# Order of weight splits in a two-stack transformer kernel: feed-forward slab 23, attention's projection slabs, a table load

## What is computed

```python
def swiglu(h, norm_g, w_in, w_out):
    u = rmsnorm(h, norm_g)
    gu = u @ w_in
    return (jax.nn.silu(gu[..., :FFN_HIDDEN]) * gu[..., FFN_HIDDEN:]) @ w_out
...
    for l in range(DEPTH):
        sh_a, sc_a, g_a, sh_f, sc_f, g_f = jnp.split(silu_c @ mod_w[l] + mod_b[l], 6, axis=-1)
        a_lat = modulate(h_lat, sh_a, sc_a)
        o_lat, o_ctx = even_mixer(...)   # l == 0: latent attention and neighbourhood attention, one projection
        # l == 1: odd_mixer, attention in windows with sinks
        h_lat = h_lat + g_a * o_lat
        h_lat = h_lat + g_f * swiglu_2(modulate(h_lat, sh_f, sc_f), ffn_w_gate_up[l], ffn_w_down[l])
```

## Time and profile before

| what | us |
|---|---|
| median of three runs | 3265.7 |
| the three runs | 3265.70, 3267.14, 3250.51 |
| profiled execution | 3255.09 |
| its span | 3253.2 |
| TensorE matmul busy | 3019.9 (93%) |
| VectorE busy | 1637.6 (50%) |
| ScalarE busy | 1157.6 (36%) |
| GpSimd busy | 263.6 (8%) |
| mean granted TensorE clock | 0.967 |

### The profile page before, as it was taken

How to read it: one execution, slowest core, us unless ns; L and a number is a source line. 1 busy time by engine, 2 the same in 40 slices (tenths; PEclk the granted TensorE clock), 3 DMA queues, 4 the chain that set the end, 5 groups by cost and what they waited for, 6 DMA issues and landing times.

```text
span 3253.2 us, 39195 instructions
## 1 busy us (share of the span) xinstructions
PE 3019.9 (93%) x15560; PEld 2529.4 (78%) x15560; DVE 1637.6 (50%) x2743; ACT 1157.6 (36%) x1927; POOL 263.6 (8%) x220
## 2 busy tenths in 40 slices
PE   7899999887888999999798999999999989999998
PEld 5678887665777788878577887888888779878887
DVE  6756665656675667651345754222222545343333
ACT  3532223434673222241345743211112345432222
POOL 2310001000561000010000100000000000000001
PEclk9999999898999999999899999999999989999999
DMA  3235444241002445431000011211121110023231
GB/s 139 85 109 162 155 156 149 75 152 34 1 1 85 149 156 175 145 120 49 33 1 12 30 35 56 66 59 64 61 66 60 63 33 1 22 83 97 92 102 66
DMA packets 75127, 260.08 MB, mean 80 GB/s; under 512 B 8129, under 2 KB 10689, under 8 KB 74817
## 3 DMA queue, kind: packets, MB, share of 16 engines
q1 hardware_dynamic: 74944, 257.57, 24.5%
HBM read 255.44 MB, written 2.10 MB: 79 GB/s over the span
## 4 chain that ended last, share of the span: by engine, by line
PE 79%; DVE 8%; ACT 7%; issue 3%; DMA 2%; DVEq 0%; SPq 0%; POOL 0%; ACTq 0%
PE PS L503 76%; PE PS L1269 2%; DVE WL L434 1%; ACT WH L428 1%; DVE SM L2258 1%; PE PS L1448 1%; ACT PTH L1520 1%; DMA RAW<-in_f_in 1%; DVE PTL L1544 1%; DVE Q L1203 0%; ACT TMP L1276 0%; DMA RAW<-in_kv_v 0%; DVE SM L1562 0%; DVE TMP L616 0%; DVE SUM L1592 0%
## 5 line engine op out<-in xcount | busy, mean ns | idle before, releaser
L503 PE MATMUL PS<-UH,WH 128*128 128x512 f32 x2296 | 873.2, 380 | 80.8 <-DVE UL L629 19.4
L503 PE MATMUL PS<-UL,WH 128*128 128x512 f32 x2296 | 860.6, 375 | 0.0
L503 PE MATMUL PS<-UH,WL 128*128 128x512 f32 x2296 | 856.6, 373 | 0.0
L428 ACT ACTIVATE WH<-RAW 128x1024 fp32r<-128x1024 f32 (+1 forms) x367 | 379.7, 1037 | 920.5 <-PE PS L503 602.3
L434 DVE TENSOR_TENSOR WL<-RAW,WH 128x1024 fp32r<-128x1024 f32 (+1 forms) x367 | 451.3, 1232 | 375.4 <-ACT WH L428 361.8
L503 PEld LDWEIGHTS PS<-UH,WH 128*128 128x128 f32 x2296 | 440.5, 192 | 173.5 <-DVE WL L434 39.9
L503 PEld LDWEIGHTS PS<-UL,WH 128*128 128x128 f32 x2296 | 440.7, 192 | 79.0 <-issue 5.6
L503 PEld LDWEIGHTS PS<-UH,WL 128*128 128x128 f32 x2296 | 439.3, 191 | 77.8
L503 PE MATMUL PS<-HH,WH 128*128 128x512 f32 x1008 | 368.9, 366 | 2.6 <-DVE HL L2128 2.6
L503 PE MATMUL PS<-HL,WH 128*128 128x512 f32 x1008 | 369.2, 366 | 0.0
L503 PE MATMUL PS<-HH,WL 128*128 128x512 f32 x1008 | 367.3, 364 | 0.0
(11 more groups left out here) (331 smaller groups left out, 4101.1 us busy)
## 6 DMA issues: line engine op xcount, KB each, us to landing
RAW<-in_mod_w SPq DMA_DIRECT2D x96, 512.0 KB, 3.5
RAW<-in_f_in SPq DMA_DIRECT2D x88, 512.0 KB, 3.5
RAW<-in_g_in SPq DMA_DIRECT2D x88, 512.0 KB, 3.4
RAW<-in_f_out SPq DMA_DIRECT2D x32, 448.0 KB, 3.9
RAW<-in_g_out SPq DMA_DIRECT2D x32, 448.0 KB, 3.2
RAW<-in_a_in SPq DMA_DIRECT2D x16, 512.0 KB, 3.8
RAW<-in_f_out SPq DMA_DIRECT2D x16, 512.0 KB, 4.3
RAW<-in_g_out SPq DMA_DIRECT2D x16, 512.0 KB, 3.4
```

The costliest lines, as they stand in the source:

```text
L428: act.e.activation(hi, raw, ACT.Copy).then_inc(wh.step(n, i), 1)
L503: return pe.e.matmul(out, l, r, start=start, stop=stop)
```

## The change

Slab 23 of a feed-forward stands ahead of the first modulations in the plan. One modulation moves from behind the last output slab of chunk 0 to behind pair 16. The split of e_out 0 to 2 moves from the start of latent attention to the end of step 46 of na on both engines; the rotary halves come ahead of the values' evacuation and the latent halves. The bias tables are issued ahead of the first slab whose place an `e_out` slab leaves, that is e_out 1, so e_out 1 to 5 are now behind the tables. The table load of the window attention comes ahead of the split of its queries. `ffn_vector` has the same two conditions as `ffn_scalar`, with `mod_step`.

```diff
@@ plan_of_weights: ffn
-        split(name + "_in", 0, 22, 1)
+        split(name + "_in", 0, 22, 1, 23)
         j = 0
         for c, n in enumerate(chunks):
             for _ in range(n):
-                split(name + "_in", *(i for i in (j, 22 + j) if i not in (0, 22, 1)))
+                split(name + "_in", *(i for i in (j, 22 + j) if i not in (0, 22, 1, 23)))
                 if step:
                     mod()
-                    if j % 3 == 0 or j == 10:
+                    if j % 3 == 0 or j in (10, 16):
                         mod()
                 j += 1
             for m in range(8):
                 plan.append((name + "_out", 8 * c + m, 128 * n, True))
-                if step and (c < 2 and m % 2 == 0 or c == 0 and m == 7):
+                if step and (c < 2 and m % 2 == 0):
                     mod()
...
@@ sync_engine
+        first_late = next(j for j, old in enumerate(slabs.old) if old is not None and slabs.plan[old][0] == "e_out")
         for j in range(3, len(slabs.plan)):
...
-            if j == after("mla_w", 0):
+            if j == first_late:
                 for h in range(8):
...
@@ even_scalar
-        high(act, "mla_w", 0)
+        rotary_high(act, 0)
         values_evac(act, 0, 0)
         values_evac(act, 0, 1)
         latent_high(act, 0, 0)
         latent_high(act, 0, 1)
-        rotary_high(act, 0)
...
@@ even_vector
-        low(dve, "mla_w", 0)
+        rotary_low(dve, 0)
         latent_low(dve, 0, 0)
         latent_low(dve, 0, 1)
-        rotary_low(dve, 0)
...
@@ na_scalar
             flips_scalar(act, s)
+            if s == 46:
+                high(act, "mla_w", 0)
...
@@ na_vector
                 na_low(dve, QU[s][0] + 1, QU[s][1])
+            if s == 46:
+                low(dve, "mla_w", 0)
...
@@ swa_scalar
+        logexp(act)
         split_queries("swa", QRAW2, lambda i: [dve_q.after("o", i + 1, "rope"), lin.after("o_in", 9)], "act", act)
-        logexp(act)
```

## The result

| | us |
|---|---|
| before, median of 20 executions | 3252.4 (3245.5 to 3269.2) |
| after, median of 20 executions | 3263.4 (3259.6 to 3274.8) |
| ratio, 95% interval | 1.0030 (1.0019 to 1.0041) |
| after, profiled execution, and its span | 3274.8, 3272.9 |
| mean granted TensorE clock | 0.960 (before: 0.967) |

The forecast was 3261 with a saving of 2.3 us, "no change". The time lies in the range and within 0.5% of before, but the direction is wrong: the kernel lost some 11 us.

A forecast was written before the change was run, and what follows sets the result against it. TensorE was taken as the bound, with 79% of the chain that ended last. Terms -4.4 - 3.0 + 3.3 - 9.8 - 2.5 + 12.8 + 1.3 = -2.3 us gave 3263.4 against the median 3265.7; 3261 was taken, range 3245 to 3274.

The forecast's parts named there:

- Feed-forward: Slab 23 ahead gains 4.4 us in f0, 3.0 in f1; the moved modulation loses 3.3 at tile 17.
- Start of latent attention: Without the projection's splits the first score comes 9.8 us earlier, and 2.5 us of clock return: gain.
- End of na: End of neighbourhood attention: the moved chain of load and splits, with half clock behind it, loses 12.8 us; bounds 8 and 16.
- three sizes: End of na: transposes 8.8 us later, 3.5 us of half clock up to the projection, 0.5 in it.
- third rival: Half clock into the projection: na costs 16, latent attention returns no clock, 3 us less gain; +6.5, 3270; 12%.
- Table load: Before the window attention: the load delays the splits of the queries, VectorE's path grows by it; loss 1.3 us.
- bounds 0 and 1.3: Least and largest loss in us allowed for the moved table load before the window attention.
- No drain: Window attention's table load: no room for the page's 1.38 us drain, which would make the loss 2.7 us.
- The base: Whole kernel: sum set against the median of three timed runs, 3265.7, 10.6 us above the profiled execution.
- The chances: Whole kernel: faster 8%, same 86%, slower 6%, with about 0.5%, or 16 us, as the limit.
- rivals 2 and 3: Rival 2: end of na hides the chain, only 3 us lost there, 3251, 13%; rival 3: the third rival, 12%.

The follow-up runs named there:

- e1: Kernel before with only slab 23 planned early and one modulation moved behind tile 16: 3249.6 us against 3254.6, ratio 0.9987.
- e8: Kernel before with only slab 23 ahead of the modulations, the modulation kept at the end of chunk 0: 3249.6 us against 3260.9, ratio 0.9968.
- e2: Kernel before with only the projection's split moved to step 46 of na, with the new operand and bias table order: 3257.4 us against 3254.6, ratio 1.0006.
- e11: Kernel before with the projection's move, but e_out 0 split inside latent attention and only e_out 1 and 2 at step 46: 3251.3 us against 3255.6.
- e13: Whole change, but the table load in front of ScalarE's wait for the last projection tile: 3254.7 us against 3251.0 before, ratio 1.0002.
- e15: Whole change run again, with a second profile: 3264.6 us against 3251.0 before, ratio 1.0035.
- e10: Kernel before with only the moved table load, written twice (one stands in the trace): 3256.6 us against 3255.6, ratio 1.0006.
- e5: Whole change run again: 3264.1 us against 3260.9 before, ratio 1.0017.
- e6: Whole change without the moved table load, which stays where it was: 3255.7 us against 3260.9 before, ratio 0.9991.
- e9: Kernel before with only the table load moved, in front of ScalarE's wait for the last projection tile: 3252.2 us against 3255.6, ratio 0.9996.
- e4: Kernel before with latent attention's new start and e_out 0 to 2 split inside it, both halves in the same step: 3258.5 us against 3254.6.
- e7: As e4, but each high half two steps ahead of its low half: 3238.4 us against 3260.9 before, ratio 0.9939.
- e14: Whole change with the moved table load written twice (one stands in the trace): 3265.0 us against 3251.0 before, ratio 1.0039.

## Why the forecast was wrong, step by step

- **Feed-forward.** Right. -4.4, -3.0 and +3.3 were -4.5, -3.3 and +3.4 (after), with the stops at the tiles that were named. Half clock behind the stop at tile 11 is an extra of 1.9 us in some executions. e1 alone gains 4.4 us by its trace and 5 by the medians, e8 shows that its 3.4 us of loss were avoidable.
- **Start of latent attention.** Right: 13.1 for 9.8 + 2.5 = 12.3. The first score comes 10.7 us earlier against the work before it, and 2.3 us more return behind it (0.8 us in e2, e11 and e13, where the gain is 11.6 in all). The window of 11 us from the first score on had a granted clock of 0.51 and has 0.84 in after:

```profile
1594.00:1605.00 11.00, 9.10 (x40) 6.31 (x40) 4.38 (x8) 5.21 (x10) 0.00 (x0) 0.84 0.00 0
```

- **End of na: mechanism right, size too small.** 12.8 was forecast and 16.2 to 16.6 came. The term had three sizes. The transposes were to be 8.8 us late and were 9.8 (1900.85 against 1905.38, and after was 14.3 us ahead at that point). The stretch from them to the projection was 1917.96 - 1905.38 = 12.6 us and was to grow by 3.5; it is 1919.30 - 1900.85 = 18.5, so it grew by 5.9. And 0.6 in the projection as forecast (0.5). TensorE was at 0.50 through all of it. The bursts, by the distances from start to start:

```profile
1908.92 1.45 PE L503 MATMUL PS<-NV,TMP 128*128 128x64 f32 x12
...
1906.14 2.66 PE L504 MATMUL PS<-NV,TMP 128*128 128x64 f32 x12
...
1909.45 2.66 PE L504 MATMUL PS<-NV,RS 128*128 128x64 f32 x12
```

  The first line is before, the two others are after. The sum had one burst of outputs at +1.2 us; two of 12 matmuls lie on this path, and they cost 1.16 and 1.17. It had four flips at +0.35; there are five at 0.42 to 0.46. Its two transposes had +0.45 and took 0.62. Together these are the 2.4 us that were not foreseen. The other 1.0 us is that the transposes came 9.8 late and not 8.8. The total is the value that the third rival gave to na (16), though its other half, that latent attention returns no clock, did not happen.
- **Table load: the step that failed.** The direct price was right (1.3; it is 1.0 to 1.1 at the first scores, 1.4 at the first maximum), and so was the reason: VectorE's chain of splits is the last wait. What failed is "bounds 0 and 1.3": the sum ended the price of the load at the first maximum and put what a later start does to the clock behind it at nothing, without a reason. The load moved the whole window attention, and inside it came 9.0 us (e15) and 15.8 us (after) at half clock. Even e10, without the long stretch, has 1.4 + 2.3 = 3.7 us by its first outputs. Between e15 and e13 the place of this one instruction is worth 9.8 us, between e5 and e6 8.4. Together with the 3.4 to 3.8 us that the end of na cost beyond its term this turns the forecast 2.3 us of gain into a loss. No rival had it; I looked for clock losses only where TensorE stood still for long, and the window attention has thin places of its own.
- **No drain.** The page ScalarE: Activation LUTs of the Trainium skill (What ACT_TABLE_LOAD costs) gives 2.66 us for a switch of set with its drain. In after the next activation starts at 2646.99, which is 0.01 us behind the end of the load at 2645.70 + 1.28. What the sum said without the drain holds at the new place as well. But this load is no switch, since the one before it (2557.96) was of the same set, and so it can't test the page's figure, neither here nor in the prediction. A real switch, from that set to the one with SiLU, stands at the start of g0 (after):

```profile
2024.17 1.28 ACT L687 ACT_TABLE_LOAD   x1
2025.46 0.81 ACT L687 ACTIVATE TMP<-PS 128x768 f32<-128x768 f32 x1
```

  SiLU begins 0.01 us behind the load's end, and the copy before the load ends at 2024.15, so the trace shows 1.3 us where the page has 2.66, and the measurement decides.
- **The base.** I had set the forecast near the median of three executions (3265.7). Of 20 executions the median is 3252.4, and the profiled one with 3255.1 was the better anchor. The base was 10.9 us too high (3263.3 less 3252.4), the change 13.3 us too low (-2.3 against +11.0). That the two nearly cancel in the absolute time (3261 against 3263.4) is luck, and so is that it lies in the range.
- **The chances.** The outer ends of rivals 2 and 3 add up to 6% and 4%, while the forecast gives 8% and 6% to faster and slower; the 2% each have no case behind them.

With the load out of the path the change is what the forecast says: 0.9991 (e6) and 1.0002 (e13) of before, neither to be told from 1. The direction was decided by the line with the smallest term.

## What to carry to other kernels

A one-microsecond term on the path deserves the same care as a ten-microsecond one when a long stage with thin places follows it: ask what idle time would hide it (here 16 us of ScalarE's, a few lines up, where e9 and e13 put it). Work that is split over two engines should be placed twice, each half in its own engine's idle time (here two steps apart); placed together, the second engine stalls for the first, here 2.5 us of stop for each slab and half clock behind it (e4), against 0.9 us for all three slabs (e7). And a chain that is moved costs its length and then the half clock that follows the stop; at the end of na the second part did not shrink with the first (5.9 us behind stops of 3.25 and of 9.08 us).

## What the runs showed of the hardware that was not expected

- TensorE stayed at 1.2 GHz while it was busy for 10.00 of 10 us in three windows in a row (after, 2800 to 2830). Work alone did not bring its clock back there; in e13 it was back one window later at the same work. The page TensorE: Matmul & The Clock Gate of the Trainium skill (HAM oscillation — how this bites in real kernels) ties such losses to waits for DMA between thin tiles. This trace does not bear that cause out: no DMA is waited for here, and the fall comes at a stop of 1.50 us that VectorE ends, in after (2790.66) and e15 (2783.31) as in e13 (2778.75). The long stay is not covered by it.
- The length of such stretches seems to change between executions of one kernel and to move a time by some 10 us: the profiled execution of e11, with a long stretch, took 3262.3 us, and the median of its 12 is 3251.3. Among 29 executions of before beside e15 the 26 lowest lie from 3246.2 to 3255.7 with a clock of 0.965 to 0.970, and three from 3265.8 to 3269.1 with 0.962 to 0.965; these have no profile, so that it is the same place that made them long is not shown.
- A table load is paid although its set is the one loaded last: before, at 2653.45, 1.28 us, with the same set loaded at 2555.71 and none between. Of two in a row one stands in the trace (e10, e14); whether the program that ran still had both is not shown.
